# A hybrid two-block network on one core: the entry of the first layer in another order

## The chip, the cores and the metric

The kernel runs on one core of one Trainium2 chip. The metric is the device time of one execution in microseconds (us); all operands lie in the chip's memory when it starts. The core has four compute engines that run their own instruction lists in order and wait for one another by semaphores: TensorE (PE in the rows; PEld is its weight load), VectorE (DVE), ScalarE (ACT) and GpSimd (POOL). SyncE (SP) only issues transfers here.

## What is computed

One sequence of 256 tokens with 1024 features (`x`), and a context of the same size (`ctx`), pass two layers of a first block and two of a second. The change touches only the start of the first layer, up to its first projection:

```python
sh_l, sc_l, ga_l = adaln(c, w_mod[layer], b_mod[layer])      # silu(c) @ w_mod + b_mod, in three parts
sh_c, sc_c, ga_c = adaln(c_ctx, w_mod[layer], b_mod[layer])
h_lat = rms_norm(x_lat, g_pre[layer]) * (1 + sc_l[:, None]) + sh_l[:, None]
h_ctx = rms_norm(x_ctx, g_pre[layer]) * (1 + sc_c) + sh_c
xv, g_hy, q, k, v, g_att = _split(h @ w_in, EVEN_SPLITS)

# hyena_filter: needed only later, by a long convolution
hdn = sin(fr * (z @ w1 + b1)); hdn = sin(fr * (hdn @ w2 + b2))
h = (hdn @ w3) * exp(-t * |deltas|)                           # taps, 512 x 1024
filt = two_sided / sum(|two_sided|)                           # then its spectrum
```

The reference works in float32.

## The kernel before

Each layer is a list of stages. A stage gives each engine a program: a Python generator that yields a time in arbitrary units and then issues some instructions. `merge` (L351 on) sorts the programs of one engine by these numbers, and that alone is the engine's instruction order; the numbers are written by hand, in the constructors at L1935 to L1941. Time 0 is the first dense matmul of the layer. So a changed number moves instructions, and never a semaphore value.

The work around the change, in the names of the rows:

- `Enter.load` (L1193) is what SP issues first: the small operands of the filter (L853), `w3` (L857), the angle and DFT tables (L859, L862, L863), the decay (L864), four halves of modulation weights (L315, 1 MB each, into the four slots of the ring `weights`), then `x` and `ctx` (L1201), 1 MB each.
- `Mods` multiplies the conditioning vectors with the 8 halves of `w_mod`, two for each of 4 chunks. A unit (L1068) is 4 matmuls of 512 columns on one half; after two units DVE (L1088) or ACT (L1079) copies the chunk's rows out; PE turns them (L1111), DVE reduces them (L1126), and behind the second and the fourth chunk makes scale and shift of features 0 to 511 and 512 to 1023 (L1138 to L1140, semaphore `mod_ready`). The slot of a half is loaded again, with the half four places on, once its unit is done; halves 8 and on are the weights of the first projection.
- `Filter`: two small layers (L870, L873) with a sine on ACT (L951) and six small DVE steps for each; DVE finishes the DFT tables (L925 to L934) with ACT (L944); 8 taps (L898), each taken out by DVE with the decay (L959); 8 spectra (L994), copied by DVE (L1015); absolute values on ACT (L969), folded by DVE (L980 to L982), summed on PE by 8 one-column products (L1002). Taps and spectra share four PSUM banks.
- `Enter`: squares of `x` and `ctx` on ACT (L1239), root (L1243), reciprocal and scaling of the four token tiles on DVE (L1252, L1254); PE turns them, one block `k` of 128 features at a time for all four tiles (L1265), into two banks in turn; ACT applies scale and shift (L1278), DVE splits the result into a leading and a remaining part (L143, L146 on `e_h`). `busy` (L1211) issues filler matmuls of the identity (L1215).
- `Feed` splits each quarter of projection weights into `qw_lead` (ACT, L334) and `qw_rest` (DVE, L146); the first dense item, 96 matmuls (L173) on four quarters, needs blocks `k` 0 and 1 with the first quarter, 2 and 3 with the second, and so on.

Of the kernel before, what the change touches and what calls it, by code (L numbers as in the profile page):

```python
# [822 lines left out]
class Filter(Stage):  # L823
# [3 lines left out]

    STEP = math.pi / (2 * SEQ)

    def __init__(self, core, room, banks, layers_at, taps_at, times, sums_at, last_at):  # L830
        self.core, self.room, self.banks, self.layers_at, self.taps_at, self.times, self.sums_at, self.last_at = core, room, banks, layers_at, taps_at, times, sums_at, last_at
        self.order = [z[1:] for z in sorted([(at, 0, n) for n, at in enumerate(taps_at)] + [(at, 1, n) for n, at in enumerate(times)])]
        s = lambda n: core.sem("hy_" + n)
        self.small_in, self.w3_in, self.decay_in, self.dft_in = s("small_in"), s("w3_in"), s("decay_in"), s("dft_in")
        self.dense, self.arg_ready, self.sined, self.filt_out = s("dense"), s("arg_ready"), s("sined"), s("filt_out")
        self.absd, self.F_done, self.F_out, self.summed, self.done, self.tabled = s("absd"), s("F_done"), s("F_out"), s("summed"), s("done"), s("tabled")
        self.folded, self.angled, self.shifted = s("folded"), s("angled"), s("shifted")
        q = room.qs
        self.absf = q[:, 0:2048].rearrange("p (t n) -> p t n", t=4)
        self.hd = q[0:64, 2048:3072].rearrange("p (i n) -> p i n", i=4)  # L840
        self.shifts = q[:, 3072:4096].rearrange("p (e i n) -> p e i n", e=2, i=2)
        self.half = core.small[:, 208:216]
        self.zt, self.w1, self.w2 = q[0:33, 4096:4352], q[0:33, 4352:4416], q[0:64, 4416:4480]
        self.ones = core.small[:, 204:208]
        self.filt = room.hs.rearrange("p (t d) -> p t d", t=4)
        self.w3, self.decay = room.qk[0:64, 0:2 * HY], room.qk[:, 2 * HY:4 * HY].rearrange("p (t d) -> p t d", t=2)
        self.snorm = core.small[:, 248:256]
        self.tensor, self.vector, self.scalar = (self.layers, self.taps, self.spectra, self.sums), (self.args, self.tables, self.tap_outs, self.totals, self.outs, self.norms, self.ends), (self.sines, self.products, self.mags)
# [3 lines left out]
        for dst, src in ((self.zt, a["z_t"]), (self.w1, a["e_filt_w1"][0]), (self.w2, a["e_filt_w2"][0])):  # L852
            eng.dma_start(dst, src).then_inc(self.small_in, 16)  # L853

    def fetch(self, eng):
        a = self.core.a
        eng.dma_start(self.w3, a["e_filt_w3"][0]).then_inc(self.w3_in, 16)  # L857
        dft = a["dft"]
        eng.dma_start(self.half[:, 0:4].rearrange("p (h n) -> p h n", h=2), dft[0:P, :].rearrange("p (h n) -> p h n", h=2)[:, :, 0:2]).then_inc(self.dft_in, 16)  # L859
        for i in range(2):  # L860
            rows = dft[i * SEQ:(i + 1) * SEQ, :].rearrange("(p e) n -> p (e n)", e=2).rearrange("p (q n) -> p q n", q=4)
            eng.dma_start(self.room.tabs[:, 2 * i:2 * i + 2].rearrange("p e h n -> p (e h) n"), rows[:, :, 0:P]).then_inc(self.dft_in, 16)  # L862
        eng.dma_start(self.ones, a["tap_ones"]).then_inc(self.dft_in, 16)  # L863
        eng.dma_start(self.decay, a["decay"].rearrange("(p t) n -> p t n", p=P)).then_inc(self.decay_in, 16)  # L864

    def layers(self, pe):
# [94 lines left out]

    def mags(self, act):
        for n, j, i in self.pieces():
            yield (self.sums_at[0] if j else self.times[0] + 0.3) + 0.1 * i
            if i == 0:
                act.wait_ge(self.filt_out, 4 * j + 4)
                if j:
                    act.wait_ge(self.folded, 1)
            self.core.nc.scalar.activation(self.absf[:, i, :], self.filt[:, i, j * BANK:(j + 1) * BANK], ACT.Abs).then_inc(self.absd, 1)  # L969
# [5 lines left out]
    def totals(self, dve):  # L975
        nc, link, z = self.core.nc, self.core.dve_chain, self.absf
        for j in range(2):
            yield (self.times[0] + 1.0, self.sums_at[0] + 5.0)[j]
            dve.wait_ge(self.absd, 4 * j + 4)
            link(dve, nc.vector.scalar_tensor_tensor(out=self.total(j), in0=z[:, 2, :], scalar=self.ones[:, 2:3], in1=z[:, 3, :], op0=ALU.mult, op1=ALU.add))  # L980
            link(dve, nc.vector.tensor_tensor(self.total(j), self.total(j), z[:, 0, :], ALU.add))
            nc.vector.tensor_tensor(self.total(j), self.total(j), z[:, 1, :], ALU.add).then_inc(self.folded, 1)  # L982
# [12 lines left out]
            mm.then_inc(self.F_done, 1)  # L995

    def sums(self, pe):
        yield self.sums_at[1]
        self.free_sums(pe)
        pe.wait_ge(self.folded, 2)  # L1000
        for k in range(KC):
            mm = self.core.nc.tensor.matmul(self.core.ps[:, 5, k:k + 1], self.total(k // 4)[:, k % 4 * P:(k % 4 + 1) * P], self.ones[:, 0:1], start=True, stop=True)  # L1002
        mm.then_inc(self.summed, 1)
# [11 lines left out]
            self.core.nc.vector.tensor_copy(self.room.F[:, f, j * BANK:(j + 1) * BANK], self.bank(1, n)).then_inc(self.F_out, 1)  # L1015

    def norms(self, dve):
        yield self.sums_at[1] + 0.8
        dve.wait_ge(self.summed, 1)
        self.core.nc.vector.reciprocal(self.snorm, self.core.ps[:, 5, 0:KC]).then_inc(self.done, 1)  # L1020

# [153 lines left out]
class Enter(Stage):  # L1175


    def __init__(self, core, room, filt, mods):
        self.core, self.room, self.filt, self.mods = core, room, filt, mods
        self.turn_at = [-11.1, -10.8, -9.2, -8.9, -2.8, -2.5, -0.9, -0.6]  # L1180
        self.idle = [(-24.5, 7), (-23.2, 10)]
        s = lambda n: core.sem("in_" + n)
        self.consts, self.x_in, self.cond_ready = s("consts"), (s("x"), s("ctx")), s("cond")
        self.squares, self.meaned, self.rooted, self.scaled = s("squares"), s("meaned"), s("rooted"), s("scaled")
# [8 lines left out]
    def load(self, sp):  # L1193
        core, a = self.core, self.core.a
        yield -60
        self.filt.fetch_small(sp)
        self.filt.fetch(sp)
        for h in range(Stream.RAW):
            core.stream.load(sp, h)
        for i, (name, at) in enumerate((("x", 0), ("ctx", LT))):  # L1200
            sp.dma_start(core.x[:, at:at + LT, :], a[name][0].rearrange("(t p) d -> p t d", p=P)).then_inc(self.x_in[i], 16)  # L1201

    def begin(self, act):
        core, a = self.core, self.core.a
# [29 lines left out]
    def stats(self, act):  # L1234
        core, nc = self.core, self.core.nc
        for t in range(NT):
            yield -16.0 + 0.05 * t
            act.wait_ge(self.x_in[t // LT], 16)
            core.act_chain(act, nc.scalar.activation(self.room.qk[:, 4096:5120], core.x[:, t, :], ACT.Square, accum_out=self.ssq[:, t:t + 1]))  # L1239
        nc.scalar.activation(self.room.qk[:, 4096:4097], self.room.qk[:, 4096:4097], ACT.Copy).then_inc(self.squares, 1)  # L1240
        yield -14.8
        act.wait_ge(self.meaned, 1)
        nc.scalar.activation(self.root, self.mean, ACT.Sqrt).then_inc(self.rooted, 1)  # L1243

    def norms(self, dve):
        core, nc = self.core, self.core.nc
        yield -14.95
        dve.wait_ge(self.squares, 1)
        nc.vector.tensor_scalar(self.mean, self.ssq, 1.0 / D, EPS, ALU.mult, ALU.add).then_inc(self.meaned, 1)
        yield -14.6  # L1250
        dve.wait_ge(self.rooted, 1)
        core.dve_chain(dve, nc.vector.reciprocal(self.rec, self.root))  # L1252
        for t in range(NT):
            nc.vector.tensor_scalar(core.x[:, t, :], core.x[:, t, :], self.rec[:, t:t + 1], None, ALU.mult).then_inc(self.scaled, 1)  # L1254
# [672 lines left out]
def even_layer(core, room):  # L1927
    nc, a, ps, first, col = core.nc, core.a, core.ps, core.stream.first, core.col
    stream = core.stream
    r = room  # L1930
# [1 line left out]
    feats = [("features", m, 0, 2 * SEQ) for m in range(4)]  # L1932


    filt = Filter(core, r, (0, 1, 2, 3), (-24.9, -23.4), [-21.9, -21.6, -21.3, -21.0, -18.7, -18.4, -16.2, -15.9], [-20.0, -17.5, -14.0, -12.4, -8.6, -5.7, -4.1, -2.2], (-13.6, 1.1), 15.4)  # L1935
    u = first["mod0"]
    mods0 = Mods(core, "m0_", r, [(0, 0), (0, 2), (0, 1), (0, 3)], range(u, u + 8), [-20.6, -18.1, -15.6, -15.0, -10.5, -9.9, -7.0, -6.4],
                 (r.qs[:, 4608:5120],), (4,), (5,), lambda pe: enter.wait_rows(pe), lambda pe: None, lags=(0.65, 2.0, 2.3), by_dve=(0, 1), turn_at=(-14.3, -13.2, -7.3, -4.4),
                 copy_at=(-17.45, -14.98, -9.25, -5.75), take_at=(-15.0, -14.7, -7.0, -4.1))
    enter = Enter(core, r, filt, mods0)  # L1940
    filt.free_sums = lambda pe: pe.wait_ge(mods0.mod_ready, 4)  # L1941

# [15 lines left out]
    u = first["e_kv"]  # L1958
    items = [Item(**span(range(u, u + 4), 0.0, 2.0), groups=tokens(BANK), src=r.h, act=kv_act, dve=kv_dve, ready_k=enter.wait_ready)]
    u = first["e_q"]  # L1960
# [46 lines left out]
    def take_head(n):  # L2007
# [5 lines left out]
        def by_dve(dve, src):  # L2013
# [4 lines left out]
    head_turn = Turn(core, "ht_", blocks, [18.0, 18.8] + [23.5 + 0.8 * n for n in range(4)] + [30.6 + 0.4 * n for n in range(4)], (6,),  # L2018
                     act=lambda n: take_head(n)[0] if n % 2 == 0 else None, dve=lambda n: take_head(n)[1] if n % 2 else None,
                     ready=lambda pe, n: pe.wait_ge(rotary.ready, 1 if n < 2 else 2 + (n - 2) // 4), free=second_free)  # L2020
    feed = Feed(core, (dense,), (mods0, mods1), prime=(-4.4, -4.3, -2.0), late=(first["e_q2"], 1.75), defer=True)
    run_stages(core, [dense, enter, filt, mods0, mods1, rotary, head_turn, feed, gate_consts, Program(gpsimd=(fetch_gates,))])
    gate_left = LeftOuts(core, "e_in_left_", dense, -2.0, 0.3)

# [1559 lines left out]
```

## Time and profile before

| | us |
|---|---|
| median of 3 runs | 1784.21 |
| lowest and highest | 1783.65, 1784.56 |
| span of the profiled execution | 1780.9 |
| outside the span (median less span) | 3.3 |
| PE busy in the span | 1732.2 |
| start of the first dense matmul | 51.53 |
| first matmul of the second dense item | 75.27 |

The profiled span runs from the first to the last instruction. The page gives busy time per engine, the span in slices with the granted TensorE clock, the chain of work that ended last, and groups of instructions; a timeline lists single stretches of one engine, with what ended the idle time before them in brackets. The start of the span, 0 to 75 us, is the stretch in which all moved instructions lie.

### The profile page before, as it was taken

How to read it: one execution, taken by the hardware profiler on the slowest of the kernel's cores; microseconds unless marked ns; L12 is line 12 of the kernel's file. 1: busy time of each engine (PE TensorE's matmuls, PEld its weight loads, DVE VectorE, ACT ScalarE, POOL GpSimd, SP SyncE). 2: the span in 40 equal slices, each digit the busy share in tenths (PEclk: the TensorE clock that was granted, in tenths of full speed). 3: DMA queues.
4: the chain of work that ended last, by engine and by line, in shares of the span. 5: the costliest groups of instructions: out<-in, count | busy, mean ns of one | idle time of the engine just before them, and what ended most of it. 6: DMA issues, size and time to landing. Idle time of an engine off the chain costs nothing. (4 is left out here: it accounts for less than half of the span.)

```text
span 1780.9 us, 22805 instructions
## 1 busy us (share of the span) xinstructions
PE 1732.2 (97%) x8527; PEld 1394.0 (78%) x8527; DVE 1164.9 (65%) x2141; ACT 914.3 (51%) x1490; POOL 49.4 (3%) x68
## 2 busy tenths in 40 slices
PE   8999999999998999999999999999999999999998
PEld 3776788777787877777777787788887787878886
DVE  6653466698437557767866775777646867577744
ACT  4333444333336356655656556467534756547743
POOL 0000000000000000000100002000000002000000
PEclk9999999999999999999999999999999999999999
DMA  9466211121425444443544444555554454555562
GB/s 333 155 200 226 95 56 64 54 70 67 142 95 175 132 125 146 147 139 107 180 147 153 147 154 155 176 177 193 198 189 157 127 175 134 183 165 183 189 218 76
DMA packets 115972, 267.23 MB, mean 150 GB/s; under 512 B 5412, under 2 KB 9837, under 8 KB 115672
## 3 DMA queue, kind: packets, MB, share of 16 engines
q1 hardware_dynamic: 111384, 252.26, 43.3%
q0 software_dynamic: 3504, 10.96, 2.0%
q10 hardware_dynamic: 976, 2.57, 0.4%
q8 instruction: 68, 1.11, 0.2%
q14 instruction: 40, 0.33, 0.1%
HBM read 264.63 MB, written 1.14 MB: 149 GB/s over the span
## 5 line engine op out<-in xcount | busy, mean ns | idle before, releaser
L146 DVE TENSOR_TENSOR qw_rest<-weights,qw_lead 128x1024 fp32r<-128x1024 f32 (+2 forms) x428 | 520.1, 1222 | 380.5 <-ACT qw_lead L334 375.3
L334 ACT ACTIVATE qw_lead<-weights 128x1024 fp32r<-128x1024 f32 (+2 forms) x428 | 446.4, 1048 | 461.5 <-PE psum L173 421.6
L173 PE MATMUL psum<-qw_lead,b_h_pair 128*128 128x512 f32 (+1 forms) x960 | 319.9, 398 | 3.3 <-ACT b_gates L2927 1.4
L173 PEld LDWEIGHTS psum<-qw_lead,b_h_pair 128*128 128x128 f32 x960 | 180.4, 188 | 43.8 <-issue 3.7
L173 PE MATMUL psum<-qw_rest,b_h_pair 128*128 128x512 f32 (+1 forms) x480 | 186.2, 388 | 0.0
L166 PE MATMUL psum<-b_h_pair,qw_lead 128*128 128x512 f32 x512 | 178.1, 392 | 2.0 <-DVE b_h_pair L713 2.0
L167 PE MATMUL psum<-b_h_pair,qw_rest 128*128 128x256 f32 x512 | 143.3, 280 | 0.0
L173 PE MATMUL psum<-e_h_lead,qw_lead 128*128 128x512 f32 x320 | 141.0, 441 | 1.8 <-DVE e_qT L1532 1.4
L173 PE MATMUL psum<-e_h_lead,qw_rest 128*128 128x512 f32 x320 | 125.7, 393 | 0.0
L173 PE MATMUL psum<-e_h_rest,qw_lead 128*128 128x512 f32 x320 | 124.9, 390 | 0.0
L166 PEld LDWEIGHTS psum<-b_h_pair,qw_lead 128*128 128x128 f32 x512 | 95.8, 187 | 23.7 <-DVE b_h_pair L713 2.9
L173 PE MATMUL psum<-qw_lead,o_h_lead 128*128 128x512 f32 x256 | 108.8, 425 | 0.3 <-PEq L120 0.3
L173 PEld LDWEIGHTS psum<-qw_rest,b_h_pair 128*128 128x128 f32 x480 | 90.6, 189 | 14.9
L173 PE MATMUL psum<-qw_lead,o_h_rest 128*128 128x512 f32 x256 | 100.1, 391 | 0.0
L173 PE MATMUL psum<-qw_rest,o_h_lead 128*128 128x512 f32 x256 | 99.9, 390 | 0.0
L173 PE MATMUL psum<-qw_lead,b_upT_rest 128*128 128x512 f32 x256 | 99.6, 389 | 0.0
L173 PE MATMUL psum<-qw_rest,b_upT_lead 128*128 128x512 f32 x256 | 99.6, 389 | 0.0
L173 PE MATMUL psum<-qw_lead,b_upT_lead 128*128 128x512 f32 x256 | 99.6, 389 | 0.0
L167 PEld LDWEIGHTS psum<-b_h_pair,qw_rest 128*128 128x128 f32 x512 | 96.8, 189 | 0.0
L173 PE MATMUL psum<-qw_lead,e_h_lead 128*128 128x512 f32 x224 | 88.4, 395 | 1.1 <-DVE e_qT L2073 1.1
L173 PE MATMUL psum<-qw_lead,e_h_rest 128*128 128x512 f32 x224 | 87.3, 390 | 0.0
L173 PE MATMUL psum<-qw_rest,e_h_lead 128*128 128x512 f32 x224 | 87.2, 389 | 0.0
(481 smaller groups left out, 3011.9 us busy)
## 6 DMA issues: line engine op xcount, KB each, us to landing
weights<-in_w_in SPq DMA_DIRECT2D x48, 1024.0 KB, 5.1
weights<-in_o_w_in SPq DMA_DIRECT2D x32, 1024.0 KB, 5.4
weights<-in_w_mlp_up SPq DMA_DIRECT2D x32, 1024.0 KB, 5.5
weights<-in_w_mlp_down SPq DMA_DIRECT2D x32, 1024.0 KB, 4.9
weights<-in_e_w_in SPq DMA_DIRECT2D x26, 1024.0 KB, 5.1
weights<-in_w_mod SPq DMA_DIRECT2D x24, 1024.0 KB, 7.1
weights<-in_e_w_out SPq DMA_DIRECT2D x8, 1024.0 KB, 4.9
weights<-in_o_w_out SPq DMA_DIRECT2D x8, 1024.0 KB, 4.9
```

The lines of the kernel that those rows point to most:

```text
L146: return eng.tensor_tensor(self.rest[at], src, self.lead[at].bitcast(F32), ALU.subtract)
L166: nc.tensor.matmul(out, lhs[0], pair, start=start, stop=False)
L167: return nc.tensor.matmul(out[:, 0:lead.shape[1]], lhs[1], lead, start=False, stop=stop)
L173: mm = nc.tensor.matmul(out, l, r, start=start and i == 0, stop=stop and i == 2)
L334: self.core.nc.scalar.activation(self.buf.lead[self.at(u)], self.raw(u), ACT.Copy).then_inc(self.lead_ready, 1)
```

## The change

No arithmetic changes, and no tile moves. SP issues its first transfers in another order. The filter's fetch is split in three. The four lists of places (`taps_at`, `times`, the modulation's `at`, `turn_at`) get new numbers; the places of the absolute values and of their folding become arguments of their own. The last four blocks that PE turns, before ahead of the dense item, get places inside it. The filler matmuls go from 7 and 10 to 4, 2 and 2.

```diff
-    def fetch(self, eng):
+    def fetch_taps(self, eng):
+        eng.dma_start(self.w3, self.core.a["e_filt_w3"][0]).then_inc(self.w3_in, 16)
+
+    def fetch_angles(self, eng):
         a = self.core.a
-        eng.dma_start(self.w3, a["e_filt_w3"][0]).then_inc(self.w3_in, 16)
         dft = a["dft"]
...
+        eng.dma_start(self.ones, a["tap_ones"]).then_inc(self.dft_in, 16)
+
+    def fetch_tables(self, eng):
...
-            yield (self.sums_at[0] if j else self.times[0] + 0.3) + 0.1 * i
+            yield self.mags_at[j] + 0.1 * i
...
-            yield (self.times[0] + 1.0, self.sums_at[0] + 5.0)[j]
+            yield self.totals_at[j]
...
-        self.turn_at = [-11.1, -10.8, -9.2, -8.9, -2.8, -2.5, -0.9, -0.6]
-        self.idle = [(-24.5, 7), (-23.2, 10)]
+        self.turn_at = [-7.0, -6.8, -5.05, -4.85, 1.0, 1.3, 2.6, 2.9]
+        self.idle = [(-20.0, 4), (-17.8, 2), (-17.0, 2)]
...
-        self.filt.fetch(sp)
-        for h in range(Stream.RAW):
-            core.stream.load(sp, h)
+        core.stream.load(sp, 0)
+        self.filt.fetch_taps(sp)
+        core.stream.load(sp, 1)
+        self.filt.fetch_angles(sp)
+        self.filt.fetch_tables(sp)
         for i, (name, at) in enumerate((("x", 0), ("ctx", LT))):
...
+        for h in range(2, Stream.RAW):
+            core.stream.load(sp, h)
...
-            yield -16.0 + 0.05 * t
+            yield (-13.6, -13.55, -12.2, -12.15)[t]
...
-    feed = Feed(core, (dense,), (mods0, mods1), prime=(-4.4, -4.3, -2.0), late=(first["e_q2"], 1.75), defer=True)
+    feed = Feed(core, (dense,), (mods0, mods1), prime=(-2.0, -1.6, -0.2), late=(first["e_q2"], 1.75), defer=True)
```

SP, from the start of the program, before (`in_w_mod` are modulation halves, `e_filt_w3` the taps' weights):

```order
L853 DMA e_qT<-in_z_t 33x256
L853 DMA e_qT<-in_e_filt_w1 33x64
L853 DMA e_qT<-in_e_filt_w2 64x64
L857 DMA e_qk<-in_e_filt_w3 64x2048
L859 DMA small<-in_dft 128x2x2
L862 DMA hy_dft<-in_dft 128x4x128 x2
L863 DMA small<-in_tap_ones 128x4
L864 DMA e_qk<-in_decay 128x2048
L315 DMA weights<-in_w_mod 128x4x512 x4
L1201 DMA x_res<-in_x 128x2x1024
L1201 DMA x_res<-in_ctx 128x2x1024
```

and after:

```order
L854 DMA e_qT<-in_e_filt_w2 64x64
L315 DMA weights<-in_w_mod 128x4x512
L857 DMA e_qk<-in_e_filt_w3 64x2048
L315 DMA weights<-in_w_mod 128x4x512
L862 DMA small<-in_dft 128x2x2
L863 DMA small<-in_tap_ones 128x4
L870 DMA hy_dft<-in_dft 128x4x128 x2
L871 DMA e_qk<-in_decay 128x2048
L1210 DMA x_res<-in_x 128x2x1024
L1210 DMA x_res<-in_ctx 128x2x1024
L315 DMA weights<-in_w_mod 128x4x512 x2
```

Two halves now stand ahead of the DFT tables and the decay, and two behind `x` and `ctx`.

PE, from its second small layer to the first spectrum, before (L1215 filler, L898 taps, L1068 a modulation unit, L994 a spectrum):

```order
L873 MATMUL psum<-e_qT 64x256 [waits hy_sined]
L1215 MATMUL psum<-ident 128x128 x10
L898 MATMUL psum<-e_qk,e_qT 128x512 [waits hy_w3_in,hy_sined]
L898 MATMUL psum<-e_qk,e_qT 128x512 x3
L1068 MATMUL psum<-weights,cond 32x512 [waits half_landed0,in_cond]
L1068 MATMUL psum<-weights,cond 32x512 x3
L994 MATMUL psum<-hT,hy_dft 128x512 [waits hy_filt_out,hy_tabled]
```

and after, with the same work at L880, L1226, L905, L1075 and L1001:

```order
L1075 MATMUL psum<-weights,cond 32x512 [waits half_landed0,in_cond]
L1075 MATMUL psum<-weights,cond 32x512 x3
L880 MATMUL psum<-e_qT 64x256 [waits hy_sined]
L1226 MATMUL psum<-ident 128x128 x2
L1075 MATMUL psum<-weights,cond 32x512 [waits half_landed1]
L1075 MATMUL psum<-weights,cond 32x512 x3
L1226 MATMUL psum<-ident 128x128 x2
L905 MATMUL psum<-e_qk,e_qT 128x512 [waits hy_w3_in,hy_sined]
L905 MATMUL psum<-e_qk,e_qT 128x512 x3
L905 MATMUL psum<-e_qk,e_qT 128x512 [waits hy_filt_out] x2
L1001 MATMUL psum<-hT,hy_dft 128x512 [waits hy_filt_out,hy_tabled]
```

Both units of the first chunk now stand ahead of the taps, and six taps instead of four ahead of the first spectrum.

DVE, around the scaling of `x`, before (L1088 copies the rows of a chunk, L1126 reduces them, L1015 copies a spectrum):

```order
L1126 TENSOR_REDUCE small<-psum 128x8 [waits m0_spread]
L1088 COPY e_qT<-psum 128x512 [waits m0_spread,chunk_done]
L1249 TENSOR_SCALAR small<-small 128x4 [waits in_squares]
L1126 TENSOR_REDUCE small<-psum 128x8 [waits m0_spread]
L1138 TENSOR_TENSOR mod<-small,cols 128x4 [waits m0_summed]
```

and after:

```order
L1265 TENSOR_SCALAR x_res<-x_res,small 128x1024 x3
L1022 COPY hy_F<-psum 128x512 [waits hy_F_done]
L1133 TENSOR_REDUCE small<-psum 128x8 [waits m0_spread]
L1022 COPY hy_F<-psum 128x512 [waits hy_F_done]
L1095 COPY e_qT<-psum 128x512 [waits m0_spread,chunk_done]
L987 SCALAR_TENSOR_TENSOR e_qT<-e_qT,small 128x512 [waits hy_absd]
```

The rows of the second chunk are now copied behind the scaling of `x`, and the first folding stands between that copy and the reduction of the same chunk.

## Rows read from the trace of the kernel before

**Rows 1.** Page: busy time by engine, share of the span, instructions

```profile
PE 1732.2 (97%) x8527; PEld 1394.0 (78%) x8527; DVE 1164.9 (65%) x2141; ACT 914.3 (51%) x1490; POOL 49.4 (3%) x68
```

**Rows 2.** PE waits from 60 us on: who for whom, us, times, longest

```profile
PE psum L173 <- DVE ga L1532: 3.8, 3, 2.5
```

**Rows 3.** PE timeline of the entry: start us, us, what, idle before it

```profile
4.01 1.08 PE L870 MATMUL psum<-e_qT 33*64 33x256 f32 x2 [4.01 <-DMA e_qT<-in_e_filt_w]
5.03 3.32 PE L1215 MATMUL psum<-ident 128*128 128x128 f32 x14
8.27 0.64 PE L873 MATMUL psum<-e_qT 64*64 64x256 f32 x2
8.85 2.50 PE L1215 MATMUL psum<-ident 128*128 128x128 f32 x20
11.85 3.71 PE L898 MATMUL psum<-e_qk,e_qT 64*128 64x512 f32 x8 [0.51 <-ACT e_qT L951]
...
25.60 1.92 PE L1068 MATMUL psum<-weights,cond 128*32 128x512 f32 x16
...
27.95 1.88 PE L994 MATMUL psum<-hT,hy_dft 128*128 128x512 f32 x4
29.67 0.60 PE L1111 MATMUL psum<-ident,e_qT 128*128 128x128 f32 x4
30.10 1.88 PE L994 MATMUL psum<-hT,hy_dft 128*128 128x512 f32 x4
34.52 1.09 PE L1265 MATMUL psum<-ident,x_res 128*128 128x128 f32 x8 [2.54 <-DVE x_res L1254]
35.55 3.56 PE L1068 MATMUL psum<-weights,cond 128*32 128x512 f32 x16
...
51.53 0.47 PE L173 MATMUL psum<-qw_lead,e_h_lead 128*128 128x512 f32 x1
...
75.27 0.39 PE L173 MATMUL psum<-qw_lead,e_h_lead 128*128 128x512 f32 x1
```

**Rows 4.** Stretches: us, PE, PEld, DVE, ACT, POOL busy; PEclk, DMA share, GB/s

```profile
4.00:8.00 4.00, 3.98 (x16) 3.24 (x16) 2.23 (x6) 0.35 (x1) 0.00 (x0) 1.00 1.07 235
...
36.00:37.00 1.00, 1.00 (x8) 0.19 (x4) 0.64 (x2) 1.00 (x3) 0.00 (x0) 0.50 1.06 389
```

**Rows 5.** DMA issues by line: what, KB each, us from issue to landing

```profile
e_qk<-in_decay SPq DMA_DIRECT2D x1, 1024.0 KB, 5.9
...
x_res<-in_ctx SPq DMA_DIRECT2D x1, 1024.0 KB, 14.0
...
e_qk<-in_e_filt_w SPq DMA_DIRECT2D x1, 512.0 KB, 4.8
hy_dft<-in_dft SPq DMA_DIRECT2D x2, 256.0 KB, 4.6
```

**Rows 6.** SP timeline of the entry: start us and length of the issues

```profile
2.19 0.59 SPq L857 DMA_DIRECT2D e_qk<-in_e_filt_w  x1
...
3.46 1.28 SPq L862 DMA_DIRECT2D hy_dft<-in_dft  x2
...
5.46 0.43 SPq L864 DMA_DIRECT2D e_qk<-in_decay  x1
...
13.27 1.23 SPq L1201 DMA_DIRECT2D x_res<-in_ctx  x1
```

**Rows 7.** DVE timeline of the entry

```profile
11.29 0.15 DVE L926 TENSOR_SCALAR small<-small 128x2 f32<-128x2 f32 x1
...
14.38 2.48 DVE L959 TENSOR_TENSOR hT<-psum,e_qk 128x512 f32<-128x512 f32 x4
...
31.73 2.74 DVE L1254 TENSOR_SCALAR x_res<-x_res,small 128x1024 f32<-128x1024 f32 x4
34.38 1.28 DVE L1015 COPY hy_F<-psum 128x512 f32<-128x512 f32 x2
```

**Rows 8.** ACT timeline of the entry: four absolute values

```profile
16.90 2.19 ACT L969 ACTIVATE e_qT<-hT 128x512 f32<-128x512 f32 x4 [3.46 <-DVE hT L959]
```

More of the change, by code:

```diff
@@ L828, with __init__ @@
     STEP = math.pi / (2 * SEQ)
-    def __init__(self, core, room, banks, layers_at, taps_at, times, sums_at, last_at):
+    def __init__(self, core, room, banks, layers_at, taps_at, times, mags_at, totals_at, sums_at, last_at):
         self.core, self.room, self.banks, self.layers_at, self.taps_at, self.times, self.sums_at, self.last_at = core, room, banks, layers_at, taps_at, times, sums_at, last_at
+        self.mags_at, self.totals_at = mags_at, totals_at
         self.order = [z[1:] for z in sorted([(at, 0, n) for n, at in enumerate(taps_at)] + [(at, 1, n) for n, at in enumerate(times)])]
@@ L853, in fetch_small @@
             eng.dma_start(dst, src).then_inc(self.small_in, 16)
-    def fetch(self, eng):
+    def fetch_taps(self, eng):
+        eng.dma_start(self.w3, self.core.a["e_filt_w3"][0]).then_inc(self.w3_in, 16)
+    def fetch_angles(self, eng):
         a = self.core.a
-        eng.dma_start(self.w3, a["e_filt_w3"][0]).then_inc(self.w3_in, 16)
         dft = a["dft"]
         eng.dma_start(self.half[:, 0:4].rearrange("p (h n) -> p h n", h=2), dft[0:P, :].rearrange("p (h n) -> p h n", h=2)[:, :, 0:2]).then_inc(self.dft_in, 16)
+        eng.dma_start(self.ones, a["tap_ones"]).then_inc(self.dft_in, 16)
+    def fetch_tables(self, eng):
+        a = self.core.a
+        dft = a["dft"]
         for i in range(2):
@@ L862, in fetch @@
             eng.dma_start(self.room.tabs[:, 2 * i:2 * i + 2].rearrange("p e h n -> p (e h) n"), rows[:, :, 0:P]).then_inc(self.dft_in, 16)
-        eng.dma_start(self.ones, a["tap_ones"]).then_inc(self.dft_in, 16)
         eng.dma_start(self.decay, a["decay"].rearrange("(p t) n -> p t n", p=P)).then_inc(self.decay_in, 16)
@@ L997, in sums @@
     def sums(self, pe):
-        yield self.sums_at[1]
+        yield self.sums_at
         self.free_sums(pe)
@@ L1017, in norms @@
     def norms(self, dve):
-        yield self.sums_at[1] + 0.8
+        yield self.sums_at + 0.8
         dve.wait_ge(self.summed, 1)
@@ L1240, in stats @@
         nc.scalar.activation(self.room.qk[:, 4096:4097], self.room.qk[:, 4096:4097], ACT.Copy).then_inc(self.squares, 1)
-        yield -14.8
+        yield -10.8
         act.wait_ge(self.meaned, 1)
@@ L1246, in norms @@
         core, nc = self.core, self.core.nc
-        yield -14.95
+        yield -10.9
         dve.wait_ge(self.squares, 1)
         nc.vector.tensor_scalar(self.mean, self.ssq, 1.0 / D, EPS, ALU.mult, ALU.add).then_inc(self.meaned, 1)
-        yield -14.6
+        yield -10.6
         dve.wait_ge(self.rooted, 1)
@@ L1932, in even_layer @@
     feats = [("features", m, 0, 2 * SEQ) for m in range(4)]
-    filt = Filter(core, r, (0, 1, 2, 3), (-24.9, -23.4), [-21.9, -21.6, -21.3, -21.0, -18.7, -18.4, -16.2, -15.9], [-20.0, -17.5, -14.0, -12.4, -8.6, -5.7, -4.1, -2.2], (-13.6, 1.1), 15.4)
+    filt = Filter(core, r, (0, 1, 2, 3), (-20.3, -18.0), [-16.2, -15.75, -15.3, -14.85, -14.3, -13.9, -12.5, -12.05], [-13.4, -11.6, -10.2, -8.7, -6.5, -4.6, -2.9, -1.6],
+                  (-11.0, -7.5), (-8.0, -3.0), 2.2, 15.4)
     u = first["mod0"]
-    mods0 = Mods(core, "m0_", r, [(0, 0), (0, 2), (0, 1), (0, 3)], range(u, u + 8), [-20.6, -18.1, -15.6, -15.0, -10.5, -9.9, -7.0, -6.4],
-                 (r.qs[:, 4608:5120],), (4,), (5,), lambda pe: enter.wait_rows(pe), lambda pe: None, lags=(0.65, 2.0, 2.3), by_dve=(0, 1), turn_at=(-14.3, -13.2, -7.3, -4.4),
-                 copy_at=(-17.45, -14.98, -9.25, -5.75), take_at=(-15.0, -14.7, -7.0, -4.1))
+    mods0 = Mods(core, "m0_", r, [(0, 0), (0, 2), (0, 1), (0, 3)], range(u, u + 8), [-18.7, -17.1, -10.7, -9.3, -7.6, -5.6, -3.7, -2.2],
+                 (r.qs[:, 4608:5120],), (4,), (5,), lambda pe: enter.wait_rows(pe), lambda pe: None, by_dve=(0, 1), turn_at=(-10.8, -7.8, -3.1, -0.7),
+                 copy_at=(-14.4, -8.6, -4.9, -1.5), take_at=(-9.1, -7.4, -2.8, -0.4))
     enter = Enter(core, r, filt, mods0)
```

## Prediction

> **What bounds the kernel now.** I read the page's busy times first, then PE's waits behind the entry, then PE's timeline of the first 75 us, and last the arrival of the first transfers. PE is busy for 97% of the span [rows 1]. Behind 60 us its longest wait in sum is 3.8 us in three parts [rows 2], so from there on the program is a row of PE work: what the entry gains or loses is carried to the end. The change moves nothing behind the first dense item, so I compare one point: the first matmul of the second dense item, at 75.27 us before [rows 3].
>
> Up to there PE loses time in four places [rows 3]: it starts at 4.01, fills up with identity products, reaches the taps at 11.85, waits 2.54 us for the scaled `x` before 34.52, and then runs two modulation units in 3.56 us that took 1.92 at 25.60. In the last the granted clock was 0.50, the lower of TensorE's two levels (1.2 GHz instead of 2.4), right behind that wait [rows 4]. The two together are 4.2 us. The filler at 5.03 has 14 instructions in 3.2 us, that at 8.85 has 20 in less than 2.5: the engine also begins at half its pace, though the clock column shows 1.00 there [rows 3, 4].
>
> **Arrivals, before and after.** The transfers queue on SP and fill the 16 engines. Before, the decay lands at 5.46 + 5.9 = 11.4 us and `ctx` at 13.27 + 14.0 = 27.3, with six transfers of 1 MB from the one to the other: 2.65 us each [rows 5, 6]. `w3` lands at 7.0 and the DFT tables by 8.7; I take 2.6 us for `w3` and 2.0 for tables and small parts, the steps between these landings. The first small operands are there at 4.0. After the change, in SP's new order: half 0 at 6.7, `w3` 9.3, half 1 at 11.95, tables 13.95, decay 16.6, `x` 19.25, `ctx` 21.9, half 2 at 24.55, half 3 at 27.2, and halves 4 and 5, whose slots are free by then, at 29.85 and 32.5. So `ctx` comes 5.4 us earlier, and the tables and the decay come 5.2 us later.
>
> **The start on PE.** First layer at 4.01; four fillers to 6.9; unit 0 at half pace to 8.8; second layer and two fillers to 9.8. Then PE waits for half 1 until 11.95; unit 1 (0.95) and two fillers end at 13.75, where the taps start: 1.9 later than before, and exactly the two units that now lie ahead of them. The nine fillers that go cost and save nothing by themselves, since PE waits there either way; what they covered is the clock, priced below. A tap costs 0.93 (3.71 for four). Six of them stand ahead of the first spectrum: 5.6 us. I take two of them at half pace, 1.9 more, because PE has just waited, and before, full pace shows only from the stretch at 8.85 on [rows 3]; none slow and all slow are the ends. The first spectrum then starts at 21.2. DVE's side is close behind: tables at 13.95, first tap out 3.1 later as before (11.29 to 14.38 [rows 7]), four taps by 19.5.
>
> **From the first spectrum to the dense item.** PE's list holds 8 spectra at 1.72 (27.95 to 29.67), 2 taps, 6 units at 0.95, 4 blocks turned at 0.5 (34.52 to 35.55 for two) and 4 chunk turns at 0.43 (29.67 to 30.10) [rows 3]: 13.8 + 1.9 + 5.7 + 2.0 + 1.7 = 25.1 us, to 46.3. No wait like the 2.54 is left, if the following hold:
> - `x` scaled: before, scaling began 4.4 us after `ctx` landed. After, two absolute values stand between, 1.1 us [rows 8]: start at 27.4, end at 30.1 with the 2.74 of [rows 7]. PE wants it at 33.7.
> - rows of chunk 1: now behind the scaling and two spectrum copies at 0.64 [rows 7] on DVE, so out at 32.1. PE wants them 11.1 us behind the start of the first spectrum (4 spectra, 2 taps, 2 units, 1 chunk turn), 32.3. This is the tightest place; both sides of it are worked out independently, and it caps what a faster start could bring.
> - scale and shift of features 0 to 511: behind the folding (three steps, about 2 us) at 35.7; ACT is then held by four absolute values that need the folding, until 36.3, and the first blocks are out at 37.4 and 38.3. PE turns the third and the fourth from 37.4 on: 0.4 us of wait.
> - first quarter of projection weights: half 8 lands at 40.5, and DVE splits the quarter by 46.9. PE wants it at 46.7.
>
> So the dense item starts at 46.9 instead of 51.53.
>
> **Inside the dense item.** Before, from its first matmul to that of the next item: 23.74 us, sums included [rows 3]. After, four blocks are turned inside it, 2.0 us: 25.7. The second scale and shift are ready at 49.6, blocks 4 and 5 at 55, wanted at 61; blocks 6 and 7 at 61.8, wanted at 66.8. Cost of the move: 2.0 us of PE work that only changes place. End at 72.6.
>
> **Sum.** 75.27 − 72.6 = 2.7 us. Span 1780.9 − 2.7 = 1778.2; with the 3.3 us outside it, 1781.5, against the median of 1784.21. The same prices applied to the kernel before, from 11.85 with its waits and slow units, give 51.1 for the 51.53: the sum may be 0.4 short. Own range of this case: 2.0 to 3.4 us of gain. What can be told from no change is about 0.2%, 3.6 us, and this forecast lies inside it.
>
> **A rule on the clock.** The rows show PE at half pace at 5.03 and at full pace at 8.85, with work in between, and a granted 0.50 behind a wait of 2.54 us [rows 3, 4]. The Trainium skill (TensorE: Matmul & The Clock Gate, Part 1: The HAM clock gate) says that the throttled state is the default and that activity releases it, and warns that the number of slow matmuls varies from run to run. This speaks against taking fillers out: after the change PE has a wait of about 2 us before half 1 and little work ahead of it. By that rule the slow pace could last over all six taps, 3.7 us more than my sum has.
>
> **Rivals.**
> - The clock stays low over the taps and beyond. Six taps at half pace instead of two: 4 × 0.93 = 3.7 later, so the item ends at 76.3 and the time is 1785.2; if only two more taps are slow, 1783.4. For it: PE now waits some 2 us ahead of 11.95, where before it had work nearly without a gap from 4.01 to 11.35. Against it: it has worked before that wait, and the wait is shorter than the 2.54 that brought the clock down. The same size of gain is lost if the slow stretch at 35.55 is not in every execution of before: gain 1.1, 1783.1. Chance of a gain of 0 to 2.0, or a loss up to 1, for such reasons: 0.18.
> - Late tables and decay: the slower side. Some 4.2 MB are queued ahead of the decay's end, in the stretch where the rate is low, 235 GB/s from 4 to 8 us [rows 4]. Each microsecond by which the decay lands behind 16.6 moves the taps' way out, all four PSUM banks and the first spectrum. From 19.3 on the gain is gone; at 235 GB/s throughout it would land at 22.1, and the time is 5.5 − 2.7 = 2.8 above, 1787.0. Against it: the slow rates belong to `w3` and the tables, which I charge at their own prices, and full-size transfers went at 389 GB/s [rows 4]. Chance 0.08.
> - Both tight sides are faster: PE at full pace for all taps (1.9 less) and `ctx` or DVE earlier by 1. Then the dense item starts at 45.3 to 46 and the gain is 3.6 to 4.5: 1780.2. Chance 0.18.
> - The entry is off the path, or moved phases later on cost more than 3.6 us: chance 0.04, most of it slower.
>
> **How the numbers follow.** Forecast 0.52. Below the 0.2% bound (under 1780.6) lie the fast rival and the lower tail of the forecast: 0.21. Above it (over 1787.8) lies the tail of the late decay and the last case: 0.04. The rest, 0.75, is within. The range runs from 1779.9, inside the fast rival, to 1784.6, which holds most of the first and leaves the late decay out.
>
> **What would show it.** In the profile after: `ctx` landing near 22 and the decay near 16.6; the first tap near 13.8 and the first spectrum near 21.2 (its distance shows how many taps were slow); no idle time above 1 us on PE from there to the dense item, and no granted 0.50; dense start near 46.9; the second item near 72.6, and the same distance at the end. It would be wrong if the first spectrum starts behind 24, if DVE's copy of chunk 1's rows ends behind 33, or if PE waits for blocks 4 to 7 inside the dense item.

## The result, and the profile after

The change made the kernel slower, by a third of a percent, where the forecast was a small gain.

| us | before | after |
|---|---|---|
| median of 5 runs each, same chip | 1784.56 | 1790.39 |
| lowest and highest | 1783.65, 1785.55 | 1788.71, 1793.53 |
| ratio, 95% interval | | 1.0035 [1.0023, 1.0048] |
| span of the profiled execution | 1780.9 | 1791.7 |

The time forecast was 1781.5, at most 1784.6. By medians the change costs 5.8 us. The two profiled executions differ by 10.8, because the one of after is the longest of its runs (1793.53), and the one of before was shorter than each of its timed runs (see the point on what lies outside the span). So the traces are read here for where time went, and the medians for how much. Of the 10.8, 9.3 are there at the second dense item already (84.57 against 75.27).

Busy time of the kernel after, first line of its page, against [rows 1], and PE's longest wait from 60 us on, against [rows 2]:

```profile
PE 1743.3 (97%) x8509; PEld 1394.8 (78%) x8509; DVE 1164.9 (65%) x2141; ACT 914.3 (51%) x1490; POOL 49.4 (3%) x68
```

```profile
PE psum L173 <- DVE ga L1543: 3.9, 3, 2.5
```

PE issues 18 instructions fewer (the nine fillers that went have two records each) and is busy for 11.1 us more. The busy times of DVE, ACT and POOL did not change. PE's busy time grew by as much as the span (11.1 and 10.8): in sum it waits no longer, and the same matmuls take longer. PE's timeline of the entry (start us, us, what, idle before it), against [rows 3], shows which:

```profile
3.78 1.08 PE L877 MATMUL psum<-e_qT 33*64 33x256 f32 x2 [3.78 <-DMA e_qT<-in_e_filt_w]
4.80 2.08 PE L1226 MATMUL psum<-ident 128*128 128x128 f32 x8
8.34 1.94 PE L1075 MATMUL psum<-weights,cond 128*32 128x512 f32 x8 [1.47 <-DMA weights<-in_w_mod]
...
11.24 1.22 PE L1226 MATMUL psum<-ident 128*128 128x128 f32 x4
13.27 1.93 PE L1075 MATMUL psum<-weights,cond 128*32 128x512 f32 x8 [0.80 <-DMA weights<-in_w_mod]
15.13 1.22 PE L1226 MATMUL psum<-ident 128*128 128x128 f32 x4
16.28 10.61 PE L905 MATMUL psum<-e_qk,e_qT 64*128 64x512 f32 x12
26.82 3.78 PE L1001 MATMUL psum<-hT,hy_dft 128*128 128x512 f32 x4
30.53 3.78 PE L905 MATMUL psum<-e_qk,e_qT 64*128 64x512 f32 x4
34.24 3.78 PE L1001 MATMUL psum<-hT,hy_dft 128*128 128x512 f32 x4
37.81 1.06 PE L1118 MATMUL psum<-ident,e_qT 128*128 128x128 f32 x4
38.80 1.10 PE L1075 MATMUL psum<-weights,cond 128*32 128x512 f32 x8
39.84 1.98 PE L1001 MATMUL psum<-hT,hy_dft 128*128 128x512 f32 x4
...
59.05 0.48 PE L173 MATMUL psum<-qw_lead,e_h_lead 128*128 128x512 f32 x1
...
84.57 0.39 PE L173 MATMUL psum<-qw_lead,e_h_lead 128*128 128x512 f32 x1
```

Read the second column for one kind of work. A modulation unit takes 1.93 at 13.27 and 1.10 at 38.80. Four records of spectra take 3.78 at 26.82 and at 34.24, and 1.98 at 39.84. Twelve of taps take 10.61, where [rows 3] had 3.71 for eight, 5.6 for twelve. All that PE does from 3.78 to about 37.8 runs at half pace, and what follows, up to the dense item, at full pace. From 13.27 on there is no idle time in brackets: PE works without a gap, and stays slow for 24 us more. The clock column doesn't tell of it. Two stretches of core 0 (columns as in [rows 4]):

```profile
16.00:20.00 4.00, 4.00 (x7) 1.70 (x7) 2.88 (x9) 1.31 (x4) 0.00 (x0) 1.00 1.01 406
20.00:28.00 8.00, 8.00 (x11) 2.86 (x10) 4.05 (x6) 7.12 (x12) 0.00 (x0) 1.00 1.04 391
```

PEclk says 1.00 while 11 matmuls fill 8 us. In these profiles the pace at the start has to be read from the durations. The 34 us are those of one execution, the longest of the five. Another of them (1790.39) has a mean granted clock of 0.991 where the other four have 0.997, so the slow stretch isn't the same, or isn't recorded the same, in each.

The other engines, against [rows 7, 8]. DVE takes out the second tap late, and the scaling of `x` and `ctx` starts at 35.60; ACT has the squares done by 25 and then waits:

```profile
20.10 0.69 DVE L966 TENSOR_TENSOR hT<-psum,e_qk 128x512 f32<-128x512 f32 x1 [0.94 <-PE psum L905]
...
35.60 2.74 DVE L1265 TENSOR_SCALAR x_res<-x_res,small 128x1024 f32<-128x1024 f32 x4
```

```profile
20.19 1.06 ACT L1250 ACTIVATE e_qk<-x_res 128x1024 f32<-128x1024 f32 x1 [2.88 <-DMA x_res<-in_x]
...
22.81 1.06 ACT L1250 ACTIVATE e_qk<-x_res 128x1024 f32<-128x1024 f32 x1 [0.29 <-DMA x_res<-in_ctx]
...
35.15 0.20 ACT L1254 ACTIVATE small<-small 128x4 f32<-128x4 f32 x1 [7.43 <-DVE small L1260]
```

The 7.43 us is a wait that follows from PE's pace: L1260 stands on DVE behind the eighth tap's way out, which PE delivered at 34.3. It delays nobody, since the scaling is done by 38.3 and PE wants the first scaled block only at 46.09.

### The profile page after: what moved, and what is told of

Same layout as the page of the kernel before. It is cut to its first block and busy times, and to the rows that moved or that the text cites. A ratio compares the mean times of both kernels' runs of the same rounds, so it can differ in the third digit from the quotient of the medians.

```text
span 1791.7 us, 22769 instructions
## 1 busy us (share of the span) xinstructions
PE 1743.3 (97%) x8509; PEld 1394.8 (78%) x8509; DVE 1164.9 (65%) x2141; ACT 914.3 (51%) x1490; POOL 49.4 (3%) x68
## 3 DMA queue, kind: packets, MB, share of 16 engines
q8 instruction: 68, 1.11, 0.2%
```

## The experiments

Two theories. **The clock**: with the fillers cut to 4, 2 and 2, the light work of the start doesn't bring TensorE to its full level, and some 34 us run at 1.2 GHz. **The order**: the later tables and decay, or the new places, cost time themselves. Each kernel was timed beside the kernel before on the same chip: e1 to e4 on one (before: 1784.89, 32 runs), the others on a second (1784.04, 27 runs). So kernels of different groups are compared by their ratios to before.

**e1: the change with more fillers.** One line:

```diff
-        self.idle = [(-20.0, 4), (-17.8, 2), (-17.0, 2)]
+        self.idle = [(-20.0, 8), (-17.8, 9), (-17.0, 2)]
```

> The changed kernel with its filler products raised from 4, 2 and 2 to 8, 9 and 2, in the same three places, so that TensorE has work through both waits for modulation halves. Theory A (the loss is the clock: TensorE stays at the lower level from 3.8 to 37.8 us because the fillers were cut): full pace by 10 to 12 us, first spectrum near 20 to 21, dense item from 47 to 48, second item near 73, time 1780.5 to 1783. Theory B (the loss is the order itself, the late tables and decay and the turns inside the dense item; the slow pace only accompanies it): the first spectrum stays behind 24, the time stays above 1787.

Measured: 1782.03 (1779.56 to 1783.97), ratio 0.9984 [0.9975, 0.9993]. PE's timeline:

```profile
5.15 3.78 PE L1226 MATMUL psum<-ident 128*128 128x128 f32 x16
8.86 1.94 PE L1075 MATMUL psum<-weights,cond 128*32 128x512 f32 x8
10.73 0.64 PE L880 MATMUL psum<-e_qT 64*64 64x256 f32 x2
11.30 2.27 PE L1226 MATMUL psum<-ident 128*128 128x128 f32 x18
13.51 1.07 PE L1075 MATMUL psum<-weights,cond 128*32 128x512 f32 x8
...
15.14 5.82 PE L905 MATMUL psum<-e_qk,e_qT 64*128 64x512 f32 x12
20.89 1.98 PE L1001 MATMUL psum<-hT,hy_dft 128*128 128x512 f32 x4
...
47.83 0.48 PE L173 MATMUL psum<-qw_lead,e_h_lead 128*128 128x512 f32 x1
...
73.38 0.39 PE L173 MATMUL psum<-qw_lead,e_h_lead 128*128 128x512 f32 x1
```

Sixteen filler records take 3.78 at 5.15 (0.24 each), eighteen take 2.27 at 11.30 (0.13 each). The clock has risen by 10.73 already, where the second layer takes 0.64, its time at full pace in [rows 3] (1.11 at half pace, in e6 below). The six taps take 5.82. The second item starts at 73.38, 11.2 before that of the change and 1.9 before [rows 3]. So the new order with enough fillers gains 1.9 us in the trace and 2.9 by medians, where 2.7 was forecast (2.0 to 3.4), and eleven more fillers turn the loss into a gain. The gain over before is 0.16%, and 1 lies outside its interval; the distance to the change is 1.0035 against 0.9984, some 9 us.

**e2: the kernel before with fewer fillers.** The converse: before's order, with two short fillers.

```diff
-        self.idle = [(-24.5, 7), (-23.2, 10)]
+        self.idle = [(-24.5, 4), (-23.2, 4)]
```

> The kernel before with its filler products cut from 7 and 10 to 4 and 4, nothing else. Theory A: the clock stays low over the taps, units and first spectra, some 10 to 20 us of work at half pace, time 1789 to 1795. Theory B, and the view that fillers only fill waits: first tap at 11.85 as before, at most 1 to 2 us lost, 1784 to 1786.

Measured: 1788.41 (1787.39 to 1790.91), 1.0024 [1.0015, 1.0033].

```profile
12.16 7.19 PE L898 MATMUL psum<-e_qk,e_qT 64*128 64x512 f32 x8 [0.93 <-ACT e_qT L951]
...
21.14 3.44 PE L994 MATMUL psum<-hT,hy_dft 128*128 128x512 f32 x4
24.51 1.99 PE L898 MATMUL psum<-e_qk,e_qT 64*128 64x512 f32 x4
```

Eight tap records take 7.19 instead of 3.71, and full pace begins at 24.5. The first dense matmul starts at 56.89, 5.4 late. The time lies 0.6 below the range that the clock theory gave, and 2.4 above that of the other. Fewer fillers make either order slower, so the effect of the clock is there without any of the moves.

**e3: the kernel before with the new transfer order.** Only SP's list changes; fillers and places stay.

```diff
-        self.filt.fetch(sp)
-        for h in range(Stream.RAW):
-            core.stream.load(sp, h)
+        core.stream.load(sp, 0)
+        self.filt.fetch_taps(sp)
+        core.stream.load(sp, 1)
+        self.filt.fetch_angles(sp)
+        self.filt.fetch_tables(sp)
...
+        for h in range(2, Stream.RAW):
+            core.stream.load(sp, h)
```

> The kernel before with the changed kernel's order of transfers, all engine orders and fillers as before. Theory A: full pace by 9 us as before, since the fillers are there; what is lost is the later decay and tables alone, first spectrum at 20 instead of 17, second item 1 to 4 us later, time 1785.5 to 1788.5. Theory B (late tables and decay are the cause): the same size of loss as the whole change, 1790 or more.

Measured: 1789.48 (1786.19 to 1791.25), 1.0026 [1.0016, 1.0035].

```profile
20.59 3.75 PE L1000 MATMUL psum<-hT,hy_dft 128*128 128x512 f32 x4 [4.14 <-DVE hT L965]
24.27 2.39 PE L904 MATMUL psum<-e_qk,e_qT 64*128 64x512 f32 x4
```

In before's places PE has done four taps and one unit by 16.4, at full pace, and waits 4.14 us for tables and decay. Behind the wait it works at half pace, and rises inside the row at 24.27. So the new transfer order alone is a loss of 4 to 5 us, more than the 1785.5 to 1788.5 that were expected of the late tables alone. The price of the half pace is in it: 3.75 and 2.39 where the rows behind take 1.98 and 1.99, some 2.2 us beside the 4.14 of the wait. In the change itself no such wait is left (above), so this isn't its cause.

**e8: e3 with 17 fillers in that wait.** It asks how much of e3's loss is clock. On top of e3's edit:

```diff
-        self.idle = [(-24.5, 7), (-23.2, 10)]
+        self.idle = [(-24.5, 7), (-23.2, 10), (-20.3, 17)]
```

> The kernel before with the changed kernel's order of transfers and 17 more fillers in the wait of 4.1 us ahead of its first spectrum, which the third experiment showed. It parts the price of the late decay from the price of the clock behind that wait. Clock theory: the first spectrum still starts near 20.6, but it and the taps behind it take 1.9 us each instead of 3.75 and 2.4, so 2 us of the 4.6 lost come back: 1786.5 to 1788. If the fillers change nothing: 1789.5.

Measured: 1788.36 (1787.01 to 1789.16), 1.0021 [1.0012, 1.003].

```profile
9.15 4.63 PE L1225 MATMUL psum<-ident 128*128 128x128 f32 x20
...
22.24 1.88 PE L1000 MATMUL psum<-hT,hy_dft 128*128 128x512 f32 x4
```

The spectrum now has full pace, but it starts at 22.24, 1.65 later than in e3. The profile isn't a clean pair with e3: here the second filler ran at half pace (4.63 for the 2.50 of e3), although the instructions up to there are the same, and with the new fillers PE came to the spectrum later than its operands. The dense item starts at 54.80 against 55.42. The time lies between the two that were expected, and the ratio fell by 0.0005, less than its interval. How much of e3's loss is clock stays open.

**e4: the change with its fillers right ahead of the taps.** (4, 2, 12) instead of (4, 2, 2).

```diff
-        self.idle = [(-20.0, 4), (-17.8, 2), (-17.0, 2)]
+        self.idle = [(-20.0, 4), (-17.8, 2), (-17.0, 12)]
```

> The changed kernel with 4, 2 and 12 fillers: the waits for the halves stay empty, ten more fillers stand in a row right ahead of the taps. Theory A in the form that identity products bring the clock up and taps and units do not: the fillers start near 15 us and take 4 to 5 us, full pace by the second or third tap, first spectrum near 23 to 25, time 1782 to 1786. Theory A in the form that the waits ahead are what counts: pace stays low as in the changed kernel, and 10 fillers at half pace come on top, 4 us: 1794.

Measured: 1784.23 (1782.65 to 1787.51), 0.9998 [0.9989, 1.0007].

```profile
14.99 3.98 PE L1226 MATMUL psum<-ident 128*128 128x128 f32 x24
18.90 5.42 PE L905 MATMUL psum<-e_qk,e_qT 64*128 64x512 f32 x12
```

The 24 records take 3.98, between 5.7 (0.24 each) and 3.0 (0.13 each): the clock rises inside them, and the taps behind run at full pace. The ten fillers more, 2.8 us in the path (3.98 less the 1.22 of four records), buy back 8.4 at the dense item (50.65 for 59.05). All ten runs are below the shortest of the change (1787.51 against 1788.71), though on another chip. It shows the direction of cause within one kernel: nothing ahead of 15 us was altered.

**e6: e1 with fillers of half height.** Same number of fillers in the same places; each multiplies 64 rows of the identity instead of 128.

```diff
-                self.core.nc.tensor.matmul(self.core.ps[:, 7, 0:P], self.core.ident[:], self.core.ident[:], start=True, stop=True)
+                self.core.nc.tensor.matmul(self.core.ps[:, 7, 0:P], self.core.ident[0:64, :], self.core.ident[0:64, :], start=True, stop=True)
```

> The changed kernel with 8, 9 and 2 fillers as in the first experiment, but each filler multiplies only 64 rows of the identity, so it keeps TensorE as long and uses half of its rows, as the taps do. If being without a wait is all that counts, full pace by 10 to 12 us and 1780.5 to 1783.5. If the kind of work counts, the half-height fillers bring the clock up late or not at all, the taps and units run at half pace and the time is 1786 to 1793.

Measured: 1791.51 (1790.23 to 1791.84, 4 runs), 1.004 [1.0025, 1.0055].

```profile
4.79 3.78 PE L1226 MATMUL psum<-ident 64*128 64x128 f32 x16
...
10.37 1.11 PE L880 MATMUL psum<-e_qT 64*64 64x256 f32 x2
11.41 4.21 PE L1226 MATMUL psum<-ident 64*128 64x128 f32 x18
15.54 1.93 PE L1075 MATMUL psum<-weights,cond 128*32 128x512 f32 x8
...
18.42 10.44 PE L905 MATMUL psum<-e_qk,e_qT 64*128 64x512 f32 x12
28.80 3.65 PE L1001 MATMUL psum<-hT,hy_dft 128*128 128x512 f32 x4
32.37 1.99 PE L905 MATMUL psum<-e_qk,e_qT 64*128 64x512 f32 x4
```

This run decides most. PE has work without a gap from 3.78 on, as e1 has from 4.14, and each filler is as long as e1's at the same pace. Yet full pace comes at 32.4 instead of 10.7, and e1's gain is gone. Being busy alone isn't what counts; the kind of work counts too. With half the rows the clock didn't rise from 4.79 to about 32; with all rows it was up at 10.73 in e1, and at the latest at 13.7 among the profiles with seven or eight fillers at the first place (e8). One profile of e6 could be chance, since e3 and e8 differ by some 5 us in this with the same instructions. But its four runs are all long (1790.23 and up), and e1's eleven all short.

**e5 and e7: fewer fillers than e1.** (7, 9, 0) and (8, 2, 2) instead of (8, 9, 2). The edit of e5, then that of e7, each against the change:

```diff
-        self.idle = [(-20.0, 4), (-17.8, 2), (-17.0, 2)]
+        self.idle = [(-20.0, 7), (-17.8, 9)]
```

```diff
-        self.idle = [(-20.0, 4), (-17.8, 2), (-17.0, 2)]
+        self.idle = [(-20.0, 8), (-17.8, 2), (-17.0, 2)]
```

> The changed kernel with 7, 9 and no fillers: the waits for the two halves are filled to their ends, and nothing delays the taps. If only a filled start matters, the taps start 0.6 to 1.1 us earlier than with 8, 9 and 2 (15.14), at full pace, and the time is 1781 to 1782.5, as that run or 0.5 better, since the rows of the second chunk cap the gain. If the clock depends on the last fillers ahead of the taps as well, part of the taps run at half pace and the time is above 1784.

> The changed kernel with 8, 2 and 2 fillers: only the first wait is filled, the one before half 1 stays. If work without a gap up to about 9 us is enough, as in the kernel before, full pace for the second layer, and 1781 to 1784. If the second wait matters as much, low clock over the taps, 1786 to 1792.

Measured: e5 1784.05 (1779.77 to 1788.15), 0.9999 [0.999, 1.0008]; e7 1782.06 (1779.46 to 1788.81), 0.9996 [0.9983, 1.0009]. Both intervals hold "no change" and overlap e1's. What differs is the spread: e5's eleven runs cover 8.4 us. Of e7's ten runs seven lie from 1779.46 to 1783.80 and three from 1788.13 to 1788.81, where e1 has eleven within 4.4 us. Its profile, of a run of the first kind:

```profile
4.88 3.47 PE L1226 MATMUL psum<-ident 128*128 128x128 f32 x16
...
12.90 1.06 PE L1075 MATMUL psum<-weights,cond 128*32 128x512 f32 x8 [2.34 <-DMA weights<-in_w_mod]
14.54 3.71 PE L905 MATMUL psum<-e_qk,e_qT 64*128 64x512 f32 x8
```

Here eight fillers were enough to raise the clock (16 records in 3.47, not 3.78), and a wait of 2.34 us didn't bring it down. Its span is 1777.7, the shortest seen. The three late runs were not profiled, but each run has a mean granted clock: 0.992 in these three, 0.995 to 0.999 in the seven. Against 0.997 that is 0.005 × 1785 = 9 us of full pace lost, where they are some 7 us late: a recorded low clock, as behind a wait, and not the unrecorded one of the start. None of the 59 runs of before falls under 0.995, while e3's, with a low stretch behind a wait in the entry, go down to 0.993. That in e7 it stood behind the 2.34 us wait is the likely reading, not a shown one. It speaks for the full waits of e1, but three late runs of ten against none of eleven are few.

The profiles show one thing more, a limit on what an earlier start can bring. In e5:

```profile
19.07 1.99 PE L905 MATMUL psum<-e_qk,e_qT 64*128 64x512 f32 x4 [1.03 <-DVE hT L966]
```

The taps start 0.8 us earlier than in e1, at 14.34, but the fifth waits 1.03 us until DVE has taken out the first. DVE starts that at 18.33 in e5 and at 18.24 in e1, straight behind its work on the late tables. The first spectrum starts at 20.99, no earlier than e1's 20.89.

## Why the prediction was wrong, point by point

| us | before | predicted | after | e1 |
|---|---|---|---|---|
| first tap | 11.85 | 13.75 | 16.28 | 15.14 |
| first spectrum | 16.97 | 21.2 | 26.82 | 20.89 |
| first dense matmul | 51.53 | 46.9 | 59.05 | 47.83 |
| second item | 75.27 | 72.6 | 84.57 | 73.38 |

- **Arrivals: right in order, forecast about 1 us too early.** Half 0 landed at 8.34 (6.7 predicted), half 1 at 13.27 (11.95), the decay at 17.6 (7.42 and 10.2 from issue to landing; 16.6), and `x` and `ctx` show at 20.19 and 22.81 on ACT (19.25 and 21.9).
- **"I take two of them at half pace": the step that failed.** The step bounded the slow stretch by the six taps ("none slow and all slow are the ends"). All six were slow, and the slow stretch neither began nor ended with them. It took in unit 1 and its fillers ahead (3.0 us where 1.8 was charged), two more taps and the spectra behind. The second item is 12.0 later than predicted: 2.5 of it are there at the first tap, 3.1 come in the six taps, and 6.5 between the first spectrum and the dense item. The distance from after to e1 at the second item, 11.2 us, is the price of the slow stretch in the profiled pair (by the ratios some 9); the prediction charged 1.9. A smaller slip stands beside it: full pace in before shows from 8.27 on, where the second layer takes 0.64 [rows 3], not only from 8.85.
- **The first rival: right mechanism, wrong size.** It named the low clock, and gave 3.7 more at most, 1785.2 for the measured 1790.39. The unfounded part was that the clock must rise once the taps are done. Nothing in the rows said so: the rows gave the pace that followed on 17 fillers, and the change took nine of them away. That "the nine fillers cost and save nothing by themselves" holds for the queue alone.
- **From the first spectrum to the dense item: right in its terms, 1.2 short.** 25.7 predicted (21.2 to 46.9), 26.9 in e1. A spectrum took 1.81 to 1.92 from start to start, where 1.72 was charged, which makes 1.0 of it. No wait above 0.24 us stands there in e1. In after it is 32.2, by the slow part.
- **Inside the dense item: right.** 25.7 predicted, 25.5 in after (59.05 to 84.57) and in e1. PE waited for none of the blocks 4 to 7.
- **Late tables and decay: a real price, not paid here.** e3 shows it in before's places, 1.0026, its share of the clock included. In the change the taps are slower than DVE takes them out, so it stays hidden; at full pace it is the limit that e5 shows.
- **Outside the span: wrong by 1.5.** I took 3.3 us, median less span. The profiled run of after has 1793.53 with a span of 1791.7, 1.8 apart. With the same 1.8, before's profiled execution took some 1782.7, under every one of the runs shown. The error is in the sum, and small beside the clock.

The Trainium skill (TensorE: Matmul & The Clock Gate, Part 1: The HAM clock gate) says that the throttled state is the default and that activity releases it. That rule spoke against the change, and the trace of after agrees, with half pace from its first matmul at 3.78. Beyond it, e6 and the change show that work of other kinds, without a gap, left TensorE at half pace until 32 and 37.8 us.

## What to carry to other kernels

Fillers at the start of a program aren't only padding for a wait: what they do to the clock is paid or earned by all the work behind them, until the clock rises. Before they are cut, price the whole stretch up to the next work that was seen to raise the clock, here up to 34 us, and not the next few matmuls. Here only fillers of full height (128 rows) did it early. Judge how many are enough by the spread of many runs: the smallest number that works in one profile (e7) need not work each time.

## What the runs showed of the hardware that was not expected

- **Half pace that no column shows.** In after PEclk is 1.00 from 16 to 28 us, while every matmul takes about twice its time.
- **Height counts.** In e1 the clock was up at 10.73, with 16 filler records of 128 rows ahead; in e6, with 38 of 64 rows in the same three places, it wasn't by 18.4. The taps of this kernel are 64 rows high, and behind a start at half pace they ran slow for 10.61 and 10.44 us. Even spectra of full height ran for 3.78 us at 26.82 in after without it rising, while in e2 and e6 it rose near the end of such a row. What decides between these isn't settled.
- **A second place, in all kernels, that moves runs by chance.** Near 570 us PE waits 2.5 us for DVE, the wait of [rows 2]. Behind it the clock may fall or not. After's row, and the stretch behind it:

```profile
577.52 0.35 PE L173 MATMUL psum<-o_h_lead,qw_lead 128*128 128x256 f32 x1 [2.53 <-DVE ga L1543]
```

```profile
578.00:585.00 7.00, 6.64 (x32) 6.24 (x31) 3.69 (x11) 4.95 (x8) 0.00 (x0) 0.52 0.44 144
```

The same place in the kernel before, and then in e5, whose row of the wait stands below them:

```profile
568.00:571.00 3.00, 2.77 (x14) 2.50 (x13) 2.07 (x9) 2.43 (x6) 0.00 (x0) 0.50 0.99 319
571.00:575.00 4.00, 4.00 (x35) 4.00 (x35) 2.48 (x7) 2.67 (x3) 0.00 (x0) 0.95 0.06 22
```

```profile
569.00:572.00 3.00, 3.00 (x27) 3.00 (x27) 1.99 (x4) 2.91 (x3) 0.00 (x0) 1.00 0.21 78
```

```profile
565.92 0.35 PE L173 MATMUL psum<-o_h_lead,qw_lead 128*128 128x256 f32 x1 [2.50 <-DVE ga L1543]
```

In after the granted clock is 0.52 over 7 us, in before 0.50 over some 3, in e5 it doesn't fall, with the same wait of 2.5 us. That is 7 × 0.48 = 3.4 us lost against 3 × 0.5 + 4 × 0.05 = 1.7 and against none, in executions that differ in nothing there. In the profile of before a third place is low, and not in that of after:

```profile
1346.00:1350.00 4.00, 3.97 (x19) 3.81 (x20) 2.41 (x5) 2.42 (x7) 0.00 (x0) 0.57 0.01 2
```

That is 4 × 0.43 = 1.7 more in before, and the two places cancel. So the recorded clock behind the entry explains none of the 10.8 between the profiled spans; the last 1.5, beyond the 9.3 of the entry, stays open but for 0.5 at a wait for modulation weights (1.7 us in after, 1.2 in before). Such places go with a part of each kernel's spread: e1's shortest run (1779.56) has a mean clock of 0.999, its longest (1783.97) 0.996. Fillers in this wait were not tried.
